# Eight-core encoder block: queue orders and PSUM banks read from tables, first weights behind the first x tile, last output in place

## The reference, cut to what matters

```python
def reference(x, ...):
    x = layer_norm(x, ln_in_g, ln_in_b)
    u = x @ w_in                                        # 1024 -> 3840
    q, k, v = u[..., :o1], u[..., o1:o2], u[..., o2:o3]
    y_a = windowed_gqa(q, k, v, rel_bias, sink) @ w_attn_out      # 128 tokens to either side
    y_c = conformer_conv(u[..., o3:o4], ...) @ w_conv_out         # GLU, depthwise 31, norm, swish
    gates = sigmoid(u[..., o4:] + b_gate)
    mix = (gates[..., :D] * y_a + gates[..., D:] * y_c) @ w_out
    x = layer_norm(ALPHA * x + mix, ln1_g, ln1_b)
    hid = silu(x @ w_gate) * (x @ w_up)
    return layer_norm(ALPHA * x + hid @ w_down, ln2_g, ln2_b)
```

## Time and profile before

| | |
|---|---|
| median of 3 runs | 895.62 us (893.24 to 897.07) |
| profiled execution, its own time | 894.11 us |
| span of its slowest core, the one read here (core 5) | 892.6 us |
| spans of the eight cores | 885.9 to 892.6 us |
| busy: PE, DVE, ACT, POOL | 98%, 56%, 31%, 21% of the span |
| DMA | 92.21 MB, mean 103 GB/s |

### The profile page before, as it was taken

How to read it: one execution, slowest core, us unless ns; L and a number is a source line. 1 busy time by engine, 2 the same in 40 slices (tenths; PEclk the granted TensorE clock), 3 DMA queues, 4 the chain that set the end, 5 groups by cost and what they waited for, 6 DMA issues and landing times.

```text
span 892.6 us, 16235 instructions; the slowest of 8 cores (885.9 to 892.6 us)
## 1 busy us (share of the span) xinstructions
PE 870.8 (98%) x5918; PEld 427.7 (48%) x5918; DVE 502.8 (56%) x717; ACT 275.6 (31%) x397; POOL 187.9 (21%) x267
## 2 busy tenths in 40 slices
PE   7999999999999999999999999999999999999995
PEld 6975543544444444444444443444444444444443
DVE  6985287977778474446253374643565445512154
ACT  4673377976563152221120011120011120011110
POOL 4111112321223233452201121211223011211000
PEclk8999999999999999999999999999999999999998
DMA  9977562760305405889965638664559036366001
GB/s 199 230 151 145 121 125 37 104 100 1 48 9 134 71 1 118 142 138 165 166 125 110 133 81 156 98 120 93 116 129 173 17 73 116 80 109 95 1 27 69
DMA packets 54206, 92.21 MB, mean 103 GB/s; under 512 B 16880, under 2 KB 23280, under 8 KB 54128
## 3 DMA queue, kind: packets, MB, share of 16 engines
q0 software_dynamic: 25488, 51.39, 38.3%
q1 hardware_dynamic: 28640, 39.78, 16.7%
HBM read 125.75 MB, written 13.63 MB: 156 GB/s over the span
## 4 chain that ended last, share of the span: by engine, by line
PE 88%; DMA 6%; DVE 2%; issue 2%; ACT 1%; POOL 0%; SPq 0%; DVEq 0%; ACTq 0%; POOLq 0%
PE ps L1448 28%; PE ps L980 19%; PE ps L1467 17%; PE ps L1385 6%; PE ps L1319 6%; PE ps L1058 3%; PE ps L1107 3%; DMA xt_54_96<-x 1%; PE ps L1229 1%; DMA out<-xE_140_182 1%; DMA xE_144_186<-x 1%; DMA out<-xE_144_186 1%; DMA xE_140_182<-x 1%; PE ps L1270 1%; PE ps L990 1%
## 5 line engine op out<-in xcount | busy, mean ns | idle before, releaser
L824 ACT ACTIVATE sgb_183_225<-ps 128x512 f32<-128x512 f32 x44 | 26.3, 598 | 223.6 <-PE ps L1448 154.9
L842 DVE TENSOR_TENSOR hid_223<-ps,sgb_182_224 128x512 bf16<-128x512 f32 x44 | 30.3, 689 | 83.1 <-PE ps L1448 83.1
L842 DVE TENSOR_TENSOR hid_223<-ps,sgb_183_225 128x512 bf16<-128x512 f32 x44 | 30.3, 688 | 74.6 <-PE ps L1448 61.1
L824 ACT ACTIVATE sgb_182_224<-ps 128x512 f32<-128x512 f32 x44 | 26.3, 598 | 143.8 <-PE ps L1448 109.4
L838 DVE SCALAR_TENSOR_TENSOR t_124_166<-gt_120_162,ps 128x512 f32<-128x512 f32 x16 | 10.8, 678 | 22.9 <-ACT gt_121_163 L824 14.4
L838 DVE SCALAR_TENSOR_TENSOR E_100_142<-ps,bias_101_143 128x1024 f32<-128x1024 f32 x15 | 18.3, 1219 | 8.2 <-PE ps L1229 3.4
L838 DVE SCALAR_TENSOR_TENSOR t_126_168<-gt_122_164,ps 128x512 f32<-128x512 f32 x16 | 10.9, 682 | 20.9 <-ACT gt_123_165 L824 14.9
L824 ACT ACT_TABLE_LOAD x12 | 15.4, 1283 | 17.1 <-DVE mv_18_60 L866 12.5
L824 ACT ACTIVATE gt_122_164<-ps,hbg_46 128x512 f32<-128x512 f32 x16 | 11.0, 687 | 30.1 <-PE ps L980 27.3
L838 DVE SCALAR_TENSOR_TENSOR E_99_141<-ps,bias_103_145 128x1024 f32<-128x1024 f32 x15 | 18.3, 1218 | 2.7 <-PE ps L1229 2.7
L838 DVE SCALAR_TENSOR_TENSOR E_98_140<-ps,bias_102_144 128x1024 f32<-128x1024 f32 x16 | 19.5, 1216 | 0.3 <-PE ps L1229 0.3
(11 more groups left out here) (787 smaller groups left out, 2062.9 us busy)
## 6 DMA issues: line engine op xcount, KB each, us to landing
xt_52_94<-x SPq DMA_DIRECT2D x4, 512.0 KB, 8.0
wE_150_192<-wg POOLq DMA_DIRECT2D x8, 256.0 KB, 9.1
wE_151_193<-wu POOLq DMA_DIRECT2D x8, 256.0 KB, 7.7
wE_146_188<-wg POOLq DMA_DIRECT2D x8, 256.0 KB, 10.9
wE_147_189<-wu POOLq DMA_DIRECT2D x8, 256.0 KB, 10.7
wE_148_190<-wg POOLq DMA_DIRECT2D x8, 256.0 KB, 7.3
wE_149_191<-wu POOLq DMA_DIRECT2D x8, 256.0 KB, 8.9
wout_174<-wout POOLq DMA_DIRECT2D x4, 512.0 KB, 12.5
```

Source lines behind the costliest of these rows:

```text
L824: sc.add("act", lambda e: e.activation(res(out), res(in_), func, **kw), reads=reads, writes=writes, cost=c, table=table, **k)
L842: sc.add(eng, lambda e: e.tensor_tensor(res(out), res(a), res(b), op), reads=reads, writes=writes, cost=dcost(n) if eng == "dve" else 0.1 ...
```

## The change

`order_queues()` and all that it needs (`RANK`, the cost constants) are gone. In their place stand two tables and a short `lay_out()`. `QUEUES` has one string per engine. A word w in it puts operation number prev + 1 + w next, where prev is the operation put last (it begins with -1), numbers being those in which `build()` adds the operations; `*n` stands for n words of 0. `BANKS` has one digit per accumulator: its first PSUM bank. An operation that opens an accumulator waits for all operations of the accumulators that held its banks before. `cost`, `wire`, `lag` and `rank` are still passed but nothing reads them.

Decoded, the tables keep every operation but put it elsewhere in its queue:

- SP begins with small, x tile 4, x tiles 0, 1, 2, 3 (before: small, x tiles 0, 1, 2, 3, 4).
- POOL begins with wA4, wA5, wA0, wA6, wA7, the root of x tile 0, wA1, wA2, wA3, then the first wQ (before: wA2, wA4, wA5, wA6, wA7, wA0, wA1, wA3).
- PE begins with the 28 warm operations; from there its order differs throughout, as do those of DVE and ACT. The first `tapw` products on DVE stand behind the LayerNorms of the first tiles.

Four edits are made to the operations themselves: `WARM` goes from 36 to 28. All eight `wA` loads wait for x tile 0 to have landed (`after=[xop[0]]`). The last tile's result goes to `xs` (its `xE` buffer) in place of `fin`, and is stored from there. The `wire` and `lag` figures of five loads change, which has no effect by itself now.

```diff
-import heapq
...
-WARM = 36
-RANK = {
...
+WARM = 28
+
+QUEUES = {
+    "pe": (
+        "10 *27 34 28 1 -23 20 -13 20 1 -2 9 -8 46 -42 1 1 -21 1 19 66 1 -2 -97 98 1 -4 -81 13 1 1 -32 32 -14 47 "
...
+    "pool": (
+        "43 1 -2 2 1 19 -24 1 1 10 16 -17 24 -29 99 -64 72 9 9 -130 174 53 9 -237 255 -256 244 104 157 -169 -11 29 "
...
+    "sp": (
+        "0 153 -154 *3 159 9 9 109 -11 19 9 74 9 -259 267 9 -186 2 -2 1 0 100 749 -528 -220 -2 -3 0 221 -120 0 2 -2 "
...
+BANKS = (
+    "01234567012345670123456701234475564021562305147444372531670475756544465464760546327624577710415446234532640145"
...
-    def order_queues(self):
...
+    def lay_out(self):
+
+        for e in self.ENGS:
+            prev = -1
+            for w in QUEUES[e].split():
+                for step in [0] * int(w[1:]) if w[0] == "*" else [int(w)]:
+                    prev += step + 1
+                    self.ops[e].append(self.all[prev])
+        assert sum(len(q) for q in self.ops.values()) == len(self.all)
+        used = [[] for _ in range(8)]
+        for op in self.ops["pe"]:
             for v in op.vts:
...
+                if v.b is None:
+                    v.b = int(BANKS[v.uid])
+                    for x in range(v.b, v.b + v.n):
+                        for o in used[x]:
                             self._dep(op, o, "war")
...
+                        used[x] = v.ops
...
-    fin, _ = sb(RA, [128, D], F32, "fin")
...
-            wop.append(castload(wA[j][:, :], win_d[ch], ["wA%d" % j], wire=1.72, lag=2.5))
+            wop.append(castload(wA[j][:, :], win_d[ch], ["wA%d" % j], wire=1.72, after=[xop[0]]))
...
-        castload(wQ[i][:, :], win_d[ch], ["wQ%d" % i], wire=1.72, lag=9.0)
+        castload(wQ[i][:, :], win_d[ch], ["wQ%d" % i], wire=1.72)
...
-            stt(fin[:, hs], xs[:, hs], rss, lnB2v[:, 1, hs], ALU.mult, ALU.add, [xr[h], rk, ("lnB2", 1)], [("fin", h)])
-            store(fin, [("fin", h)], 512 * h, 512 * h + 512)
+            stt(xs[:, hs], xs[:, hs], rss, lnB2v[:, 1, hs], ALU.mult, ALU.add, [xr[h], rk, ("lnB2", 1)], [xr[h]])
+            store(xs, [xr[h]], 512 * h, 512 * h + 512)
...
-    sc.order_queues()
+    sc.lay_out()
```

More of the change, by code:

```diff
@@ L36 @@
 GW = 542
-WARM = 36
-RANK = {
-    "#margin": 0.6039, ("#late", "act"): 4.2315, ("#late", "dve"): 3.7922, ("#late", "pe"): 1.6861,
[87 rows of a table removed]
-    ("loadAO", "pool"): -0.4466, ("loadC", "pool"): 130.7329, ("loadG0", "pool"): 408.2262,
[67 rows of a table removed]
-}
+WARM = 28
+QUEUES = {
[19 rows of a table added]
+    "act": (
[11 rows of a table added]
+    "dve": (
[21 rows of a table added]
+    "pool": (
[14 rows of a table added]
+}
+BANKS = (
+    "01234567012345670123456701234475564021562305147444372531670475756544465464760546327624577710415446234532640145"
+    "64325774662333200204046764060202657644545004101016044501213322423022061206026244524610453123112564363766705734"
+    "25063526262402400064660626246644606032024000031644511032046302367206310456276037723271103740167310743610373264"
+    "10237756246240473050302324044007207276376304235463025000207642035406407403052053655032057706760452132001553012"
+    "61306755135637530133671033157556063313711365375604131645731261404235763607132450530043671052345454457176036732"
+    "2345454501540101076671102")
 T_EXP = "exp"
@@ L255 @@
     NSLOT = {"sp": 16, "pool": 16}
-    HOP = 0.14
-    PIPE = {"dve": 0.07, "act": 0.08}
-    DMA_HEAD = {"sp": 0.8, "pool": 1.0}
-    DMA_TAIL = 2.0
-    MARGIN = RANK.get("#margin", 0.3)
-    LATE = {e: RANK.get(("#late", e), 0.0) for e in ("pe", "act", "dve")}
-    LATE_FROM = 60.0
-    SHARE = {"sp": 1.0, "pool": 1.2}
-    TURN_RATE = 0.22
-    DMA_FIRST = {"sp": 0.0, "pool": 5.0}
-    BEGIN = 1.1
-    FETCH_N = 256
-    FETCH_US = 7.0
-    HOLDERS = ("s",)
-    CAPS = {"warm": 1, "lnt": 2, "glu": 4, "kvq": 2, "conv": 4, "stat": 2, "s": 4, "pv": 2, "ot": 1,
-            "gt": 2, "y": 2, "mix": 2, "ht": 1, "gu": 4, "down": 4}
     def __init__(self):
@@ L318, in add @@
             op.order[o] = True
-        op.rank = RANK.get(self.group, self.cur) + RANK.get((self.group, eng), 0) if rank is None else rank
+        op.rank = self.cur if rank is None else rank
         for r in reads:
@@ L915, in build @@
     stage("first", -100)
-    load(small[:, :], small_d, ["small"], wire=0.9)
-    xop = [xload(0, wire=2.0)]
+    load(small[:, :], small_d, ["small"], wire=1.1)
+    xop = [xload(0)]
     xop += [xload(t) for t in range(1, 4)]
```

233 lines of the change are left out of this document (removed), and 214 rows, old and new, of tables (QUEUES, RANK).

## The result

The changed kernel takes 890.01 us (median of four runs, 889.36 to 891.03), the kernel before beside it 894.88: a ratio of 0.9945 (95% interval 0.9919 to 0.9971). The forecast was 890.1. The profiled execution took 889.36 us.

What follows compares the result with a forecast made beforehand. Matmul time on PE was taken as the bound, leaving queue order only its idle places. Head 1.0, feed-forward 3.0, attention 1.1 and tail 0.4 sum to 5.5 us: 895.6 to 890.1, range 884.5 to 896.5.

Steps and rivals of the forecast that it cites:

- signs of being wrong: wA4 after 19 us, gate and up matmuls waiting for wE at 390 to 450, or new PE waits at 60 to 200.
- Head, 1.0 us: Start of the kernel: PE's unbroken work would begin at 21.5 us in place of 22.5, gaining 1.0 us.
- the latest, 21.5, holds: Head: with first weights landing 3.2 us apart from 16.0, the latest start any of them allows, 21.5 us, sets PE's start.
- within what the weights hold up anyway: Head: PE's low clock costs up to two pieces, hidden because late weights hold PE up anyway.
- Rival (d): Head: the weights' wait for x tile 0 does nothing, only the order gains; counted inside the forecast case, chance 0.50.
- (c): Head: weights issued late land late, so the kernel gets slower, 900 us if the first lands at 24; chance 0.10.
- Feed-forward, 3.0 us: 500 to 700 us: longer distances behind reloaded tiles and weight loads regain 3.0 of PE's 4.0 us idle.
- the distance to what stands behind the reloaded tile: Feed-forward: matmul work from a `down` to PE's first need behind the reload; under 28 us for four of eight, then two.
- Rival (b): Feed-forward: the stalls only move, 3 to 5 us come back at 390 to 450 us, giving 894 to 896; chance 0.23.
- the swapped banks cost nothing by themselves: Changed PSUM banks only alter which product a matmul waits for; priced at nothing, uncovered a wait such as 1.8 us.
- Attention, 1.1 us: 140 to 200 us: more work between `pv` and the transposes needing its normalised result regains 1.1 of 2.6 us idle.
- Tail, 0.4 us: End of the kernel: writing the last output in place removes VectorE's idle time before its last two products, 0.42 us.

Runs made afterwards that it cites:

- the moves: Changed kernel with eight operations moved by a place or a few in the PE, ScalarE and VectorE queues; ratio 0.9940 to the kernel before.

## Why the prediction was right, and where not

The total is right (890.0 for 890.1), but that it is so close is luck. The sum started from 895.6, the median of three executions; beside the changed kernel the kernel before took 894.9, so 4.9 us were gained and not 5.5, and by the 51 executions (893.1 in their median) nearer 3. The terms are not all right either, and their errors cancel. Of its signs of being wrong two of three came: waits for wE at 438 us on four cores, and new waits between 60 and 200 us.

- **Head, 1.0 us:** 1.3. The first weight was put at 16.0 and landed at 15.1 to 16.8. The next two came at 17.3 to 18.7 and 19.0 to 20.6, not 3.2 us apart, so the step "the latest, 21.5, holds" fails: PE waited 0.5 us for weights, in the mean of the cores. What held the pieces is the step taken too lightly, the low clock "within what the weights hold up anyway": filling the gaps gave 1.4 us. Rival (d), that the wait does nothing, had been put inside the forecast, since "x0 lands at 10.2 either way"; without the wait it lands at 11.7 and x3 at 21.6. The step looked at the 0.01 MB before 6 us and not at what the weights take after that. (c) fell: issuing late was the gain. The Trainium skill's advice in "DMA: Bandwidth & Descriptors", "Rules for kernel authors", to issue early and wait late, did not hold here, where the early transfers shared the DMA engines with tiles that were needed first; the measurement decides, by 3.7 us in the new order.
- **Feed-forward, 3.0 us:** 1.8 gained from 480 us on, 1.1 lost between 200 and 480, 0.7 net. The mechanism, the distance to what stands behind the reloaded tile, was right: the run without the stores shows that the late reload is the cause, and reloads became no faster. On core 5 a store and the reload behind it take 8 to 19 us in the changed kernel, 13.7 in the mean of the eight, against 6 to 20 and 10.4 before; VectorE still stands at some of them, but from 480 us on PE loses only 0.5 us in place of 2.3:

```profile
669.45 1.28 DVE L510 SCALAR_TENSOR_TENSOR xE_140_182<-xE_140_182,mvA_50,lnA_73 128x1024 f32<-128x1024 f32 x1 [4.36 <-DMA xE_140_182<-x]
...
690.48 1.28 DVE L510 SCALAR_TENSOR_TENSOR xE_143_185<-xE_143_185,mvA_50,lnA_73 128x1024 f32<-128x1024 f32 x1 [1.43 <-DMA xE_143_185<-x]
```

  Of the two distances left under 28 us one stalls (0.4 us at 672, in the mean of the cores). But a distance alone picks the wrong tiles. Before, two of the eight lie under 28 and not four (25 and 23, tiles 10 and 14), and those did not stall, since store and reload took 6 us; tiles 11 and 15, at 31 and 28, did, with 20 and 19. Rival (b) came in part, for a weight at 438 us (0.55 in the mean); its own sum is off, 890.1 with 3 to 5 us more is 893 to 895. The 1.0 us at 375, a bank still held by VectorE, was in no list: "the swapped banks cost nothing by themselves" was priced at nothing. Whether the new bank or the new order makes that wait was not told apart.
- **Attention, 1.1 us:** 0.1 or none. Counting how far `pv` stands from its transposes priced one wait; the stage has little slack on VectorE and ScalarE (busy 51 and 50 of 60 us), and a wait taken away there comes back at the next group, as the moves showed.
- **Tail, 0.4 us:** 1.4. The 0.42 of VectorE was right (0.35 with `fin` back). Not seen: SP's waits ahead of the first store (0.3), and 0.7 from the order of the last row of waits, a by-product of x4 standing ahead of x0.
- **Against the slowest core:** terms were read on the core with the largest stalls of one execution, whose gains are larger than the mean: 7.4 us on that core, 3.7 in the mean. That the slowest core gains more than the mean (3.2 against 2.5 by all executions) is in line with this, but was not taken apart.

## What to carry to other kernels

Read each stage on all cores, as lateness against uninterrupted work: on one core, or in one execution, a term of a microsecond can be chance. Holding back a transfer was worth more here than issuing it early (3.7 us of the head), since it shares the DMA engines with what is needed first; the order of the queues had to fit, for either without the other gave nothing or lost. And look at the very end of a program: the row of semaphore waits around the last store cost 0.85 us here, and an output tile that overlies old ones 0.8.

## Not expected

PE stops in the middle of a row of matmuls that needs no semaphore. In the changed kernel core 0 has such a stop, and the clock is at 0.52 behind it:

```profile
29.96 0.22 PE L730 MATMUL ps<-x0T_34_76,wA_46_88 128*128 128x128 bf16 x1 [2.57 <-issue]
```

The kernel before has one on the same core, with the clock at 1.00 behind it:

```profile
28.34 0.62 PE L1058 MATMUL ps<-x0T_34_76,wA_46_88 128*128 128x128 bf16 x8 [1.89 <-issue]
```

Lateness grows by 4.4 us around the stop in the changed kernel and by 2.1 before; that is most of why this core is not shorter. Its queues from 26 to 30 us, in the changed kernel:

```profile
q0 software_dynamic: 177, 0.32, 52.7%
q1 hardware_dynamic: 174, 0.65, 49.9%
q8 instruction: 1, 0.02, 1.5%
q14 instruction: 1, 0.01, 1.1%
```

Instruction packets move while the weights and x tiles fill the DMA engines. Queue q8 brings some 48 packets of 16 KB to each core, most of them without a stop; but the 13 traces hold 34 stops of 0.5 us or more without a semaphore behind the first 16 us, and every one ends 0.9 to 1.6 us after a packet of q8 is through. With eight warm operations more a stop stood inside one convolution row on all eight cores; with six more it was not there. So its place goes with the number of instructions ahead of it. That PE waits for its instructions there is what these times say; no run held the instructions apart from the load of the DMA engines.
